# Using all four quadrants of the array in a batched triangular solve

## The reference, cut to what matters

```python
def step(state, inp):
    r_t, w_t, k_t, v_t, a_t, b_t = inp
    sa = jnp.einsum('bhij,bhj->bhi', state, a_t)
    state = (state * w_t[:, :, None, :] + sa[..., None] * b_t[:, :, None, :]
             + v_t[..., None] * k_t[:, :, None, :])
    y_t = jnp.einsum('bhij,bhj->bhi', state, r_t)
    return state, y_t
```

## Time and profile before

| | |
|---|---|
| median of 3 runs | 1086.36 us (1084.11 to 1094.11) |
| the profiled execution, its own time | 1084.71 us |
| its span | 1082.9 us |
| granted TensorE clock, mean | 0.99 |
| busy, share of the span | PE 94%, PEld 62%, DVE 50%, ACT 31%, POOL 13% |
| the solve with its forms | about 208 to 327 us |

### The profile page before, as it was taken

One profiled execution on the slowest core, in us unless ns is written; L12 is line 12 of the kernel. 1 busy time (PEld: TensorE's weight loads), 2 busy tenths in 40 slices (PEclk: granted clock), 3 DMA queues, 4 the chain that ended last, 5 costly groups with the idle time before them and its releaser, 6 DMA issues.

```text
span 1082.9 us, 19397 instructions
## 1 busy us (share of the span) xinstructions
PE 1020.6 (94%) x8536; PEld 670.2 (62%) x8536; DVE 545.4 (50%) x807; ACT 331.5 (31%) x567; POOL 140.0 (13%) x158
## 2 busy tenths in 40 slices
PE   4999999999898989999999899999999999999998
PEld 3977799999795668878788334444444434443333
DVE  4658871265645648476756524333343334333445
ACT  6477753033236762321433111111111111111110
POOL 0000000283973350000000100000000000000000
PEclk9899999999999999999999999999999999999999
DMA  9631221000004036666386799999999999999993
GB/s 364 233 117 39 78 77 44 2 14 5 4 5 156 8 137 202 226 214 228 131 342 240 281 419 426 427 427 427 426 425 427 425 427 428 427 426 426 428 425 129
DMA packets 44805, 273.27 MB, mean 252 GB/s; under 512 B 7168, under 2 KB 7312, under 8 KB 30768
## 3 DMA queue, kind: packets, MB, share of 16 engines
q1 hardware_dynamic: 41312, 264.42, 60.5%
q0 software_dynamic: 2400, 4.28, 1.2%
q10 hardware_dynamic: 1008, 3.31, 0.8%
HBM read 272.00 MB, written 4.19 MB: 255 GB/s over the span
## 4 chain that ended last, share of the span: by engine, by line
PE 74%; DMA 16%; ACT 4%; DVE 3%; issue 1%; POOL 1%; SPq 0%; DVEq 0%; ACTq 0%; POOLq 0%
PE banks L1623 29%; PE banks L2101 15%; DMA w_ring<-in_w 7%; PE banks L2115 7%; DMA w_tok<-in_w 3%; DMA w_qkv<-in_w 3%; DMA h_table<-w_qkv 2%; PE banks L1778 2%; PE banks L2139 1%; PE banks L1780 1%; PE banks L1793 1%; PE banks L2088 1%; PE banks L2107 1%; ACT xT L859 1%; PE banks L2140 1%
## 5 line engine op out<-in xcount | busy, mean ns | idle before, releaser
L1531 DVE TENSOR_TENSOR hid<-banks,silu_a 64x512 f32<-64x512 f32 x32 | 22.2, 693 | 211.5 <-ACT silu_a L864 211.5
L2115 PE MATMUL banks<-w_ring,hidT 128*64 128x512 f32 x512 | 116.9, 598 | 0.0
L2101 PE MATMUL banks<-w_tok,xT 128*64 128x512 f32 x176 | 79.5, 605 | 5.2 <-DMA w_ring<-in_w 5.2
L864 ACT ACTIVATE silu_a<-banks 64x512 f32<-64x512 f32 x32 | 18.9, 591 | 208.2 <-PE banks L2102 208.2
L1518 DVE SCALAR_TENSOR_TENSOR mod<-banks,row_weight,mod 64x512 f32<-64x512 f32 x64 | 47.9, 748 | 68.2 <-PE banks L2115 67.2
L2101 PE MATMUL banks<-w_ab,xT 128*64 128x512 f32 x176 | 77.8, 595 | 4.4 <-DMA w_tok<-in_w 3.2
L2102 PE MATMUL banks<-w_ring,xT 128*64 128x512 f32 x176 | 79.6, 606 | 0.0
L2102 PE MATMUL banks<-w_tok,xT 128*64 128x512 f32 x176 | 77.9, 596 | 0.0
L1525 DVE TENSOR_TENSOR x<-x,banks 128x1024 f32<-128x1024 f32 x60 | 71.8, 1219 | 8.7 <-PE banks L2140 8.2
L2115 PEld LDWEIGHTS banks<-w_ring,hidT 128*64 128x64 f32 x512 | 34.0, 136 | 66.2 <-issue 66.1
L1623 PE MATMUL banks<-x_r,ring_r 128*128 128x512 f32 x192 | 74.9, 390 | 0.0
(11 more groups left out here) (381 smaller groups left out, 2357.1 us busy)
## 6 DMA issues: line engine op xcount, KB each, us to landing
w_ring<-in_w SPq DMA_DIRECT2D x52, 2048.0 KB, 31.7
w_tok<-in_w SPq DMA_DIRECT2D x22, 2048.0 KB, 30.4
w_ab<-in_w SPq DMA_DIRECT2D x11, 2048.0 KB, 27.3
w_qkv<-in_w SPq DMA_DIRECT2D x10, 2048.0 KB, 32.7
ada_buf<-in_w_ada SPq DMA_DIRECT2D x64, 256.0 KB, 3.2
tokm<-in_w_gate SPq DMA_DIRECT2D x3, 2048.0 KB, 14.1
ring<-in_w_mix SPq DMA_DIRECT2D x5, 1024.0 KB, 4.7
ring<-in_w_ada SPq DMA_DIRECT2D x2, 2048.0 KB, 15.0
```

The lines of the kernel that those rows point to most:

```text
L864: act.activation(silu_a[:, :], bank[2][0:SLOTS, :], ACT.Silu).then_inc(silu_done, 1)
L1531: dve.tensor_tensor(hid[:, :], bank[3][SLOTS:P, :], silu_a[:, :], ALU.mult).then_inc(hid_v, 1)
L2101: pe.matmul(bank[2][0:SLOTS, :], rows, w1[:, k, :], start=(k == 0), stop=(k == KT - 1))
L2115: mm = pe.matmul(bank[5][SLOTS * n:SLOTS * n + SLOTS, :], hidT[:, k, :], w2[:, k, 512 * n:512 * n + 512], start=(k == 0), stop=(k == 3))
```

## The change

Three things are changed in the solve.

- In "p" the product is written to the other partition half, so PP lies on the half opposite to T and INV, and INVT is kept there too. Then "nm" reads both its operands from the other half; its product for INV is written back to the own half of bank a_, and its product for INVT to the other half of bank b_ (columns 0 to 256 of each). ACT copies 2 x 256 columns out of the two banks. "m5" writes the final INVT to the own half.
- INVT of the first level is made from a transposed copy that PE makes: "t0" has a second set of products, with the identity as the stationary operand, from T to the other half of b_ (columns 256 to 512), and m0 on DVE masks that from PSUM. "x" now comes before "t0", "t0" of a group waits for ACT's copy of "x", "p1" waits for m0, and DVE does n0 and m0 of one group before the next group.
- "q" is no longer an event. Its products are made inside "gh" between the two products for h. queries_added waits for "gh".

```diff
-        MM_EVENTS = ["ab", "t0", "x"] + LEVELS + ["wu", "gh", "q"]
+        MM_EVENTS = ["ab", "x", "t0"] + LEVELS + ["wu", "gh"]
...
-                            src, dst = a_[:, :], group_part(k, 1024, 512, 8)
-                        act.activation(dst.rearrange("p h n -> p (h n)"), src, ACT.Copy).then_inc(solve_a[k], 1)
+                        if ev[0] == "n":
+                            act.activation(group_part(k, 1024, 512, 2), banks[k][:, :, 0:256], ACT.Copy).then_inc(solve_a[k], 1)
...
-                dve.wait_ge(solve_mm[k], mm_at(half, "q"))
+                dve.wait_ge(solve_mm[k], mm_at(half, "gh"))
...
-                for ev in V_EVENTS[3:-1]:
-                    for k in range(NG):
+                starts = [(ev, k) for k in range(NG) for ev in ("n0", "m0")]
+                for turns in [starts] + [[(ev, k) for k in range(NG)] for ev in V_EVENTS[5:-1]]:
+                    for ev, k in turns:
...
-                            ins = dve.tensor_tensor(INVT[k], FORMS[k][:, 0], bc4("level0_t"), ALU.mult)
+                            ins = dve.tensor_tensor(INVT[k], f4(b_[:, 256:512]), bc4("level0_t"), ALU.mult)
...
+                    if ev == "t0":
+                        for rows, other in halves:
+                            pe.matmul(a_[rows, at], FORMS[k][rows, 0, i, :], eye[rows, :], start=True, stop=True)
+                        for rows, other in halves:
+                            mm = pe.matmul(b_[other, beside], eye[rows, :], FORMS[k][rows, 0, i, :], start=True, stop=True)
...
+                    elif ev[0] == "p":
+                        for rows, other in halves:
+                            mm = pe.matmul(b_[other, at], FORMS[k][rows, 0, i, :], INV[k][rows, i, :], start=True, stop=True)
+                    elif ev[0] == "n":
+                        for rows, other in halves:
+                            pe.matmul(a_[rows, at], INVT[k][other, i, :], PP[k][other, i, :], start=True, stop=True)
+                        for rows, other in halves:
+                            mm = pe.matmul(b_[other, at], PP[k][other, i, :], INVT[k][other, i, :], start=True, stop=True)
+                    elif ev == "m5":
+                        for rows, other in halves:
+                            mm = pe.matmul(a_[rows, beside], PP[k][other, i, :], INVT[k][other, i, :], start=True, stop=True)
...
+                    else:
+                        for rows, other in halves:
+                            pe.matmul(a_[rows, at], WU[k][rows, i, 0:HD], tokm[rows, sc, ct, 1, hc], start=True, stop=True)
+                        for rows, other in halves:
+                            pe.matmul(b_[other, at], tokm[rows, sc, ct, 1, hc], WU[k][rows, i, HD:P], start=True, stop=False)
+                        for rows, other in halves:
+                            pe.matmul(a_[rows, beside], WU[k][rows, i, 0:HD], FORMS[k][rows, 2, i, :], start=True, stop=True)
+                        for rows, other in halves:
                             mm = pe.matmul(b_[other, at], tokm[rows, sc, ct, 2, hc], tokm[rows, sc, ct, 0, hc], start=False, stop=True)
...
-                            if half == 0 and ev == "t0" and k < NG - 1:
+                            if half == 0 and ev == "x" and k < NG - 1:
                                 between(bank[2 * k][:, 256:256 + P], 6)
+                            if ev == "t0":
+                                pe.wait_ge(solve_a[k], a_at(half, "x"))
                         elif ev == "p1":
-                            pe.wait_ge(solve_v[k], v_at(half, "n0"))
-                            pe.wait_ge(solve_a[k], a_at(half, "x"))
+                            pe.wait_ge(solve_v[k], v_at(half, "m0"))
```

More of the change, by code:

```diff
@@ L711, in _ @@
                             src, dst = a_[:, 256:512], INVT[k]
-                        else:
-                            src, dst = a_[:, :], group_part(k, 1024, 512, 8)
-                        act.activation(dst.rearrange("p h n -> p (h n)"), src, ACT.Copy).then_inc(solve_a[k], 1)
+                        if ev[0] == "n":
+                            act.activation(group_part(k, 1024, 512, 2), banks[k][:, :, 0:256], ACT.Copy).then_inc(solve_a[k], 1)
+                        else:
+                            act.activation(dst.rearrange("p h n -> p (h n)"), src, ACT.Copy).then_inc(solve_a[k], 1)
                 for n in range(4):
@@ L1216, in _ @@
             for half in range(2):
-                for ev in V_EVENTS[3:-1]:
-                    for k in range(NG):
+                starts = [(ev, k) for k in range(NG) for ev in ("n0", "m0")]
+                for turns in [starts] + [[(ev, k) for k in range(NG)] for ev in V_EVENTS[5:-1]]:
+                    for ev, k in turns:
                         a_, b_ = bank[2 * k], bank[2 * k + 1]
                         sc, g = 2 * half + k // 2, k % 2
-                        if ev != "m0":
-                            dve.wait_ge(solve_mm[k], mm_at(half, {"n0": "t0", "g": "gh"}.get(ev, ev)))
+                        dve.wait_ge(solve_mm[k], mm_at(half, {"n0": "t0", "m0": "t0", "g": "gh"}.get(ev, ev)))
                         if ev == "n0":
@@ L1765, in solve_step @@
                     ct, odd = head_of(k, i)
[L1766 to L1794, removed]
-                            mm = pe.matmul(b_[rows, P * i + HD:P * i + P], INVT[k][rows, i, :], XX[k][rows, i, :], start=True, stop=True)
-                        elif ev == "gh":
-                            mm = pe.matmul(b_[other, at], Bt, WU[k][rows, i, HD:P], start=True, stop=False)
@@ L1798, in solve_step @@
-                    if ev == "gh":
-                        for c in range(2):
-                            rows, other = slice(CH * c, CH * c + CH), slice(CH * (1 - c), CH * (1 - c) + CH)
+                    hc, at, beside = slice(HD * odd, HD * odd + HD), slice(CH * i, CH * i + CH), slice(256 + CH * i, 256 + CH * i + CH)
+                    halves = [(slice(CH * c, CH * c + CH), slice(CH * (1 - c), CH * (1 - c) + CH)) for c in range(2)]
+                    eye = const("eye2")
+                    if ev == "t0":
[3 more added lines that the diff above has]
+                            mm = pe.matmul(b_[other, beside], eye[rows, :], FORMS[k][rows, 0, i, :], start=True, stop=True)
+                    elif ev == "x":
+                        for rows, other in halves:
+                            mm = pe.matmul(b_[rows, at], FORMS[k][rows, 1, i, :], tokm[rows, sc, ct, 0, hc], start=True, stop=True)
+                    elif ev[0] == "p":
[9 more added lines that the diff above has]
+                            mm = pe.matmul(a_[rows, beside], PP[k][other, i, :], INVT[k][other, i, :], start=True, stop=True)
+                    elif ev == "wu":
+                        for rows, other in halves:
+                            pe.matmul(b_[rows, P * i:P * i + HD], INVT[k][rows, i, :], tokm[rows, sc, ct, 3, hc], start=True, stop=True)
+                        for rows, other in halves:
+                            mm = pe.matmul(b_[rows, P * i + HD:P * i + P], INVT[k][rows, i, :], XX[k][rows, i, :], start=True, stop=True)
+                    else:
+                        for rows, other in halves:
+                            pe.matmul(a_[rows, at], WU[k][rows, i, 0:HD], tokm[rows, sc, ct, 1, hc], start=True, stop=True)
+                        for rows, other in halves:
+                            pe.matmul(b_[other, at], tokm[rows, sc, ct, 1, hc], WU[k][rows, i, HD:P], start=True, stop=False)
+                        for rows, other in halves:
+                            pe.matmul(a_[rows, beside], WU[k][rows, i, 0:HD], FORMS[k][rows, 2, i, :], start=True, stop=True)
+                        for rows, other in halves:
@@ L1861, in _ @@
                         elif ev == "nm1":
-                            pe.wait_ge(solve_v[k], v_at(half, "m0"))
                             pe.wait_ge(solve_v[k], v_at(half, "p1"))
@@ L1867, in _ @@
                             pe.wait_ge(solve_a[k], a_at(half, "m5"))
-                        elif ev == "gh":
+                        else:
                             pe.wait_ge(solve_a[k], a_at(half, "wu"))
-                        else:
-                            pe.wait_ge(solve_v[k], v_at(half, "g"))
                         solve_step(half, k, ev)
```

## The result

The changed kernel takes 1094.92 us (median of 20 runs, 1089.49 to 1100.77) against 1085.45 (20 runs, 1082.33 to 1094.11): ratio 1.0086, 95% interval 1.007 to 1.0102. It is slower by 9.5 us, where the forecast was no change, and 0.9 us above the range of 1076 to 1094. The profiled execution took 1095.88 us with a span of 1094.1.

What follows compares the result with a forecast made beforehand. PE's solve, its levels just under the instruction-fetch limit, bounds the changed stretch. First half +1.7, middle -1.0, second half's fetching: net +0.1 us, put on the 1086.36 median: 1086.5 us, range 1076 to 1094.

Steps and rivals of the forecast that it cites:

- q moved into gh: Query products inside gh, their own stage removed: gain 0, 128 instructions (1.8 us) per half moved ahead of gh(3)'s end.
- rival 3: Quadrants do not overlap as ordered: levels stay at 5.60 us, +5 to +6 us in all, 1092 us; chance 0.03.
- The fetching decides the levels: Solve's levels: quadrants alone would allow 3.73 us, but fetching 384 instructions at 71 a us needs 5.4 us.
- One block per 3.6 us: PE's instruction queue: 256 instructions fetched per 3.6 us, 71 a us, with 3.5 and 3.74 as bounds.
- about 5.4 (5.2 to 5.6): Time in us of one level of the solve after the change, against 5.60 before.
- m0 at 0.35: First level's mask on DVE, read from PSUM: 0.35 us each, with 1.24 as the other bound.
- ACT's copies out of two banks: Level evictions of 2 x 256 columns: 0.50 us each, four 2.0 us per level, hidden under the level's 5.4.
- First half +1.7: Solve to the end of the first half's gh: 1.7 us later, with 256 more instructions ahead of gh(3)'s end.
- Second half -0.6: Solve from the last mask of the second half's forms to its g(3): 0.6 us shorter.
- The middle's -1.0: Between the halves: a 1.0 us fetch stop at 271.7 goes, as PE has 128 fewer instructions there: -1.0 us.
- Rival 1: The fetcher keeps up with 103 instructions a us, so quadrants decide: -16.4 us, 1070 us; chance 0.13.
- Rival 2: Fetching gets dearer without pauses, 4.2 us per 256 instructions: 12.6 us more, 1099 us; chance 0.05.

Runs made afterwards that it cites:

- the padded kernel: Changed kernel plus ten identity products (six first half, four second) on PE between the last gh of a half and chain: 1086.99 us, ratio 0.9994 to the kernel before.
- the pair with halved instructions: Changed kernel and kernel before, each with p and nm products made for two heads at once, inverse left out: 1084.21 and 1080.02 us; levels 3.50 and 5.24 us.

## Why the prediction was wrong, and where it was right

**The step that failed** is "q moved into gh": "the removed stage was covered ... Gain 0". The work was covered indeed, and DVE's sequence ended where the prediction put it. But the cover was looked at from one side only. The q products were also what PE did while DVE was the one that counted, and the prediction gave no price to PE being idle there. The parts were all there: a stop for fetching forecast inside gh(3), and DVE's 2.8 us behind it, now with nothing on PE. Their sum (5.3 us with 1.10 busy, after) was never written down, and neither was what the solve would cost at half the granted clock. The runs showed in place of "Gain 0" a loss of some 9 us: the padded kernel spares 3.7 us in the middle (20.8 against 17.1) and 4.1 at the end (14.7 against 10.6), and 1.45 in the norm's first products. No rival had this mechanism; rival 3 named a number near it (1092) for a reason that the traces exclude.

**What held.** The fetching decides the levels: foretold from three stops, shown by 17 of them, with 128 + 128 instructions or a multiple from one to the next within each half, and by the pair with halved instructions. One block per 3.6 us: 3.55 measured where packets follow one another. A level at "about 5.4 (5.2 to 5.6)" came to 5.25 in the first half and 5.1 to 5.5 in the second; with q back the second half had 5.3 to 5.8. "15 to 20 us" of issue idle: 17.7. One packet more. m0 at 0.35: 0.33 to 0.34 between starts. ACT's copies out of two banks: four in 2.06 us, with 0.48 to 0.50 between starts, the pitch of one bank (0.50). First half +1.7: +1.9. Second half -0.6: -1.3. The middle's -1.0, hidden in the result, comes out as -0.7 in the padded kernel.

**The rivals.** Rival 1 (the fetcher keeps up, 1070 us) falls with the stops; that the array would allow it is shown by the 3.50 us level. Rival 2 (4.2 us a block) falls with 3.55; the three seven-slice spacings on which it leaned (4.03 us) are the coarseness of the view in part, since of the six spacings between packet starts only one, of 4.14 us, is over 3.8. Rival 3 falls with 14.6 ns a record, measured in nm, where n writes both partition halves of bank a_ and m both of bank b_.

**What stays open.** The last 3 us or so after the solve in the profiles (760.2 against 755.3, less the norm) were not taken apart; the padded kernel shows 757.3 there. Nor was it tried how much idle time PE may have before chain, so no limit can be given; the same idle in the second half was followed by the fall in one profile (after) and not in another (only q moved).

## What to carry to other kernels

Before removing or moving covered work on PE, write down how long PE will then stand idle at that place, stops for fetching included, and price what follows at half clock; here ten products that nobody reads were 7.9 us cheaper than the gap. The levels of this kernel, many small products, were bound by the supply of their instructions once four quadrants were in use (256 per 3.55 us): divide PE's instructions by the spacing of the instruction queue's packets before counting on a faster array, and put two products with one stationary operand into one.

## What the runs showed of the hardware

- After 5.3 us with PE busy for 1.10 the granted clock was 0.50 for 10.2 us; at the second place, after 7.08 us with 4.08 busy, for 13.7 us; with only q moved, after 6.1 us with 1.98 busy, for 13.65. After 5.15 us with 3.78 busy (padded) it stayed at 1.00. The clock records of all twelve profiles show no other value than 1.00 and 0.50.
- Where PE was short of instructions, the packets of its 256 stood 3.28 to 3.8 us apart (mean 3.55 in the view above, 72 a us), while four quadrants with 64-column products take 137 a us (the forms of a group before: 64 loads, with as many matmuls, in 0.93 us from 208.27).
- A product from the other partition half, or one written to it, went at the same pace as one within a half (14.6 ns a record with all four quadrants, 29.2 with two).
